# Three reorderings between VectorE and GpSimd in a one-core float32 network: the scan loop of the Mamba stage, the last mix of two mixers, the last mean square

## The reference

```
uA = head_rms_norm(oA, hg_norm_g) * silu(hz)
uB = head_rms_norm(oB, ret_norm_g) * silu(rz)
m  = sigmoid(ga) * uA + sigmoid(gb) * uB
x  = x + gate * (m @ w_out)
out = rms_norm(x, final_g)
```

```
y = y_diag + y_off + d_skip * xs
y = y * silu(z)                        # then a norm over each group of 256 channels
```

## Time and profile before

| | us |
|---|---|
| median of 3 runs | 1345.24 (1345.16 to 1345.25) |
| the profiled execution's own time | 1344.97 |
| its span | 1343.2 |
| PE busy | 1331.4 |
| DVE, ACT, POOL busy | 958.1, 753.4, 213.1 |

### The profile page before, as it was taken

The page is one execution under the profiler, slowest core; times in us unless marked ns, Lnnn a source line. Parts: engine busy times, 40 slices in busy tenths (PEclk is TensorE's granted clock), DMA queues, the critical chain, the costliest instruction groups (busy, mean ns, idle before and its releaser), DMA issues.

```text
span 1343.2 us, 21456 instructions
## 1 busy us (share of the span) xinstructions
PE 1331.4 (99%) x8527; PEld 1156.6 (86%) x8527; DVE 958.1 (71%) x1026; ACT 753.4 (56%) x882; POOL 213.1 (16%) x199
## 2 busy tenths in 40 slices
PE   9999999999999999999999999999999999999997
PEld 7888888888888888888899988888888899888886
DVE  6666668867666676666677999767888756877586
ACT  6444455656444454444566678854444465657453
POOL 3400001101000020000000026220000001655740
PEclk9999999999999999999999999999999999999999
DMA  8655546525555565555544564488887544655341
GB/s 279 209 188 189 195 159 208 188 92 191 187 187 187 188 189 189 187 187 187 188 157 162 188 207 172 145 278 294 286 285 236 187 158 157 220 160 184 113 156 49
DMA packets 158292, 254.19 MB, mean 189 GB/s; under 512 B 8784, under 2 KB 99232, under 8 KB 156560
## 3 DMA queue, kind: packets, MB, share of 16 engines
q1 hardware_dynamic: 155136, 232.94, 53.1%
q0 software_dynamic: 2576, 18.45, 3.7%
q10 hardware_dynamic: 512, 1.85, 0.4%
HBM read 252.12 MB, written 1.08 MB: 189 GB/s over the span
## 4 chain that ended last, share of the span: by engine, by line
PE 89%; issue 7%; DVE 2%; ACT 1%; DMA 1%; POOL 0%; POOLq 0%; DVEq 0%; ACTq 0%
PE psum L656 24%; PE psum L644 13%; PE psum L688 5%; PE psum L689 5%; PE psum L690 5%; PE psum L1951 4%; PE psum L1952 4%; PE psum L1953 4%; PE psum L428 3%; PE psum L429 3%; PE psum L435 3%; PE psum L463 1%; PE psum L471 1%; PE psum L465 1%; PE psum L1496 1%
## 5 line engine op out<-in xcount | busy, mean ns | idle before, releaser
L391 DVE TENSOR_TENSOR w_lo<-raw,w_hi 128x2048 fp32r<-128x2048 f32 x220 | 512.3, 2331 | 203.2 <-ACT w_hi L383 203.0
L383 ACT ACTIVATE w_hi<-raw 128x2048 fp32r<-128x2048 f32 x220 | 420.6, 1912 | 173.1 <-PE psum L690 78.5
L656 PE MATMUL psum<-hT,w_hi 128*128 128x512 f32 x1408 | 335.9, 390 | 0.6 <-DVE hT L527 0.4
L656 PEld LDWEIGHTS psum<-hT,w_hi 128*128 128x128 f32 x1408 | 260.7, 188 | 53.8 <-issue 1.2
L644 PEld LDWEIGHTS psum<-hT,w_lo 128*128 128x128 f32 x1408 | 180.2, 191 | 6.6
L644 PE MATMUL psum<-hT,w_lo 128*128 128x256 f32 x1408 | 183.0, 283 | 0.0
L688 PE MATMUL psum<-w_hi,hidT_hi 128*128 128x512 f32 x320 | 125.1, 391 | 0.0
L689 PE MATMUL psum<-w_lo,hidT_hi 128*128 128x512 f32 x320 | 125.0, 391 | 0.0
L690 PE MATMUL psum<-w_hi,hidT_lo 128*128 128x512 f32 x320 | 124.5, 389 | 0.0
L533 POOL TENSOR_SCALAR meansq<-sumsq 128x2 f32<-128x2 f32 x7 | 5.9, 836 | 659.8 <-ACT xn L501 659.8
L738 ACT ACTIVATE hid<-psum 128x512 f32<-128x512 f32 x44 | 26.3, 598 | 149.8 <-PE psum L644 149.8
(11 more groups left out here) (387 smaller groups left out, 1996.6 us busy)
## 6 DMA issues: line engine op xcount, KB each, us to landing
raw<-in_ffn_w_up SPq DMA_DIRECT2D x88, 512.0 KB, 4.8
raw<-in_ffn_w_down SPq DMA_DIRECT2D x88, 512.0 KB, 4.3
raw<-in_ffn_w_gate SPq DMA_DIRECT2D x86, 512.0 KB, 4.7
raw<-in_w_in SPq DMA_DIRECT2D x72, 512.0 KB, 4.6
raw<-in_ssm_w_in SPq DMA_DIRECT2D x48, 512.0 KB, 4.6
raw<-in_attn_w_qkv SPq DMA_DIRECT2D x24, 512.0 KB, 4.7
ada_in<-in_w_ada POOLq DMA_DIRECT2D x8, 1536.0 KB, 8.3
raw<-in_ssm_w_out SPq DMA_DIRECT2D x16, 512.0 KB, 4.3
```

The source lines that it names most:

```text
L383: act.activation(w_hi[:, slot, :], raw[:, slot, :], ACT.Copy).then_inc(sem("hi_ready"), 1)
L391: dve.tensor_tensor(w_lo[:, slot, :], raw[:, slot, :], w_hi[:, slot, :].bitcast(F32), ALU.subtract)\
L656: pe.matmul(both, hi[:, k, at_:at_ + P], hT[:, k, :, :], start=k == 0, stop=False, skip_group_check=True)
```

## The change

- Start: `first_lo` no longer raises a semaphore for its first three pieces, on which nothing waited.
- Scan loop, DVE: in pair j = 1 the `split_lo` stands behind the weighing and no longer ahead of the finishing.
- Scan loop, POOL: the second of the two early gatings of y is issued at item 11, behind that item's `xdt` and `x_skip`, and no longer at item 10.
- Last mix, DVE: out_b is multiplied by gate_b for both halves at once, behind the head squares of tick 25 (`gate_second`) and ahead of the head factors and the sigmoid. `mix` is then: out_b by the sigmoid, out_a plus out_b. The head factors for the second half are applied in tick 26, ahead of that tick's split, and no longer in tick 27.
- Last mean: DVE adds the two sums of squares and epsilon in one instruction for each token half, and POOL only takes the power.

```diff
--- before.py
+++ after.py
@@ -1015,8 +1015,7 @@
                     dve.wait_ge(sem("first_hi"), k + 1)
                 else:
                     dve.wait_ge(sem("hi_ready"), 1)
-                dve.tensor_tensor(w_lo[:, 0, cs], raw[:, 0, cs], w_hi[:, 0, cs].bitcast(F32), ALU.subtract)\
-                   .then_inc(sem("first_lo" if k < 3 else "lo_ready"), 1)
+                return dve.tensor_tensor(w_lo[:, 0, cs], raw[:, 0, cs], w_hi[:, 0, cs].bitcast(F32), ALU.subtract)
 
             hT_lo_tiles(dve, 0, ("ffn1_norm", 0), (0, 1))
             first_lo(0)
@@ -1024,7 +1023,7 @@
             hT_lo_tiles(dve, 0, ("ffn1_norm", 0), (2, 3))
             first_lo(2)
             hT_lo_tiles(dve, 0, ("ffn1_norm", 0), (4, 5))
-            first_lo(3)
+            first_lo(3).then_inc(sem("lo_ready"), 1)
             hT_lo_tiles(dve, 0, ("ffn1_norm", 0), (6, 7))
             split_lo(dve, 1)
             split_lo(dve, 2)
@@ -1734,8 +1733,8 @@
                     load_cum(1)
                 if i == 10:
                     group_rstd(0)
-                if i in (7, 10):
-                    q = (i - 7) // 3
+                if i in (7, 11):
+                    q = (i - 7) // 4
                     cs = slice(512 * q, 512 * (q + 1))
                     pool.wait_ge(sem("y"), 4 * (q + 1))
                     pool.wait_ge(sem("z_silu"), q + 1)
@@ -1864,11 +1863,14 @@
             for j in range(1, ITEMS // 2):
                 differences(2 * j)
                 differences(2 * j + 1)
-                split_lo(dve, FIRST_UNIT["ssm_z"] + j - 1 + SLOTS)
+                if j > 1:
+                    split_lo(dve, FIRST_UNIT["ssm_z"] + j - 1 + SLOTS)
                 finish(2 * j - 2)
                 finish(2 * j - 1)
                 weigh(2 * j)
                 weigh(2 * j + 1)
+                if j == 1:
+                    split_lo(dve, FIRST_UNIT["ssm_z"] + SLOTS)
                 if j == 6:
                     lo_of_y(0)
             split_lo(dve, FIRST_UNIT["ssm_z"] + ITEMS // 2 - 1 + SLOTS)
@@ -2289,13 +2291,9 @@
             head_rstd_pool(pool, 1)
             pool.wait_ge(sem("gained"), 4)
             pool.dma_start(gain_row[:, :], w["final_g_2"][0].partition_broadcast(P)).then_inc(sem("gain_in"), 16)
-            order = in_order(pool, "gpsimd_order")
-            pool.wait_ge(sem("sumsq"), 4 * 7 + 2)
-            order(pool.tensor_scalar(meansq[:, :], sumsq[:, 0, :], 1.0, EPS, ALU.mult, ALU.add))
             for t in range(TT):
                 ts = slice(t, t + 1)
-                pool.wait_ge(sem("sumsq"), 4 * 7 + 2 + t + 1)
-                order(pool.tensor_tensor(meansq[:, ts], meansq[:, ts], sumsq[:, 1, ts], ALU.add))
+                pool.wait_ge(sem("mean"), t + 1)
                 pool.tensor_tensor(rstd[:, ts], meansq[:, ts], neg_half[:, ts], ALU.pow).then_inc(sem("rstd"), 1)
 
         def across_tokens(row):
@@ -2366,13 +2364,14 @@
                 if i < TICKS - 2:
                     second_dve_tick(dve, i)
                 c = NT + i // 2
+                if i == TICKS - 2:
+                    normed(dve, 1, out_b, None, (1,))
                 if i == TICKS - 1:
                     lo_of_m(dve, 0)
-                    normed(dve, 1, out_b, None, (1,))
                     mix(dve, c, 1)
                 split_lo(dve, u + 2 * NT + i + SLOTS)
                 if i % 2 and GA <= CHUNKS2[c] < GB:
-                    gate(dve, c)
+                    gate_first(dve, c)
                 if i == TICKS - 3:
                     normed(dve, 1, out_b, None, (0,))
                     mix(dve, c, 0)
@@ -2395,6 +2394,11 @@
                         dve.tensor_tensor(scaled[:, t, cs], x[:, t, cs], gain_row[:, cs], ALU.mult)\
                            .then_inc(sem("gained_x"), 1)
             for t in range(TT):
+                ts = slice(t, t + 1)
+                dve.wait_ge(sem("sumsq"), 4 * 7 + 2 + t + 1)
+                dve.scalar_tensor_tensor(meansq[:, ts], sumsq[:, 0, ts], EPS, sumsq[:, 1, ts], ALU.add, ALU.add)\
+                   .then_inc(sem("mean"), 1)
+            for t in range(TT):
                 dve.wait_ge(sem("rstd"), 8 + t)
                 dve.scalar_tensor_tensor(xn[:, t, cs], x[:, t, cs], rstd[:, t:t + 1], gain_row[:, cs],
                                          ALU.mult, ALU.mult).then_inc(sem(f"final_{t}"), 1)
@@ -2404,14 +2408,18 @@
             dve.tensor_tensor(hT_lo[:, k, :], h_tmp[:, k, :], hT_hi[:, k, :].bitcast(F32), ALU.subtract)\
                .then_inc(sem("hT"), 1)
 
-        def gate(dve, c):
-
-            n = 2 * (CHUNKS2[c] >= GB) + CHUNKS2[c] % D // 512
-            to = (gate_b if n >= 2 else gate_a)[:, :, 512 * (n % 2):512 * (n % 2 + 1)]
+        def gate_first(dve, c):
+
+            n = CHUNKS2[c] % D // 512
+            to = gate_a[:, :, 512 * n:512 * (n + 1)]
             dve.wait_ge(sem("in2_out"), c + 1)
-            if n >= 2:
-                dve.wait_ge(sem("gained"), n + 1)
             dve.tensor_tensor(to, to, sig[:, :, :], ALU.mult).then_inc(sem("gated"), 1)
+
+        def gate_second(dve):
+
+            order = in_order(dve, "vector_order")
+            dve.wait_ge(sem("gained"), 4)
+            order(dve.tensor_tensor(out_b[:, :, :], out_b[:, :, :], gate_b[:, :, :], ALU.mult))
 
         def lo_of_m(dve, half):
             for k in range(4 * half, 4 * half + 4):
@@ -2422,11 +2430,10 @@
         def mix(dve, c, half):
 
             cs = slice(512 * half, 512 * (half + 1))
-            gate(dve, c)
-            order = in_order(dve, "vector_order")
+            b = out_b[:, :, cs]
+            dve.wait_ge(sem("in2_out"), c + 1)
+            dve.tensor_tensor(b, b, sig[:, :, :], ALU.mult).then_inc(sem("gated"), 1)
             dve.wait_ge(sem("gated"), 3 + half)
-            b = out_b[:, :, cs]
-            order(dve.tensor_tensor(b, b, gate_b[:, :, cs], ALU.mult))
             dve.tensor_tensor(out_a[:, :, cs], out_a[:, :, cs], b, ALU.add).then_inc(sem("m"), 1)
 
         def normed(dve, a, buf, other, halves=(0, 1)):
@@ -2506,6 +2513,7 @@
                 normed(dve, 0, out_a, gate_a)
             if i == OUT_B + 1:
                 head_squares(dve, 1, square_b)
+                gate_second(dve)
 
         block = ctx.enter_context(nc.Block())
         FFN1 = ("ffn1_w_gate", "ffn1_w_up", "ffn1_w_down")
```

## The result

| | before | after |
|---|---|---|
| median of the runs timed side by side | 1344.82 us (1344.03 to 1345.61, 12 runs) | 1348.93 us (1346.82 to 1350.15, 12 runs) |
| ratio | 1 | 1.0029, interval 1.0021 to 1.0037 |
| profiled execution, time and span | 1344.97, 1343.2 us | 1348.74, 1346.9 us |

The kernel became slower by 4.1 us. The forecast was 1347.0, or 1.8 more than before, with 1348.0 as its upper end. So it missed: the sign was right, the size about half. The twelve times lie in two groups: four from 1346.82 to 1347.26, eight from 1348.53 to 1350.15. The profiled execution is of the upper group.

A forecast was written before the change was run, and what follows sets the result against it. PE was taken as the bound, busy 1331.4 of 1343.2 us. Loop -0.4, mix +2.2 and mean 0 gave +1.8 on 1344.97, so 1346.8; the median stands 0.27 higher, so 1347.0, range 1343.4 to 1348.0.

The forecast's parts named there:

- Start: Kernel start: three raised semaphores fewer, with nothing waiting on them, worth 0.
- POOL held up by DVE in the last mix: Last mix: DVE's added product and a split delay POOL's scale and power; first turn 2.71 us later; chance 0.62.
- The two rivals with a lower price: Last mix: POOL not held up, 1344.3 or 1343.1 us, chance 0.16; only its scale held up, 1344.9 us, chance 0.12.
- The sum of the mix, +2.2: Last mix: first turn 2.71 us later, second turn's 0.52 us stall gone; +2.2 us, bounds -0.5 and +2.4.
- The scan loop, -0.4: Scan loop: 0.86 us of possible gain less 0.5 of slips, -0.4 us; bounds a 1.6 gain and a 0.6 loss.
- A and B: Scan loop PE stalls expected to go: scores at 795.38, 0.67 us idle; outputs at 828.89, 0.34 us late.
- The cap from DVE's weighing: Scan loop's end: DVE runs without pause to the weighing ending at 843.95, so the loop gains at most 0.86 us.
- ACT's squares as its next reader, which are a pair away: Scan loop: POOL's later gating delays nobody, since its next reader on ACT comes a pair later.
- The slips: Scan loop: earlier POOL xdt products stretch DVE's differences, delaying DVE; two slips, 0.5 us in all.
- Last mean, 0: Last mean: moving additions from POOL to DVE leaves the end unchanged, 0, between -0.1 and +0.15 us.
- The slower rival: Scan loop becomes DVE's limit through slips in pairs 2 to 6: +2.7 us or more, 1347.9 to 1348.3; chance 0.10.
- stall C: Last mix: PE idles 0.52 us before the second turn at 1318.23; expected to go, -0.52 us.

The follow-up runs named there:

- one-operand: Changed kernel with the out_b by gate_b product replaced by two tensor_reduce of gate_b, similar length, one operand read, output lacking that factor: 1345.24 us.
- gate-behind: Changed kernel with the out_b by gate_b product put behind tick 25's split, so POOL makes the head factors first: 1346.27 us.
- mix alone: Kernel before with only the last mix's edits, scan loop and mean as before: 1347.14 us; profiled again three times.
- the kernel with the ten matmuls: Changed kernel plus ten 128x512 matmuls whose result nobody reads, put on PE ahead of the wait for the first turn: 1347.51 us.
- copy-first kernel: scan-only kernel with ACT's last copy of z ahead of the second quarter's squares instead of behind them: 1345.61 us.
- scan-only kernel: Kernel before with only the scan loop's two edits (weighing ahead of split, gating behind item 11's xdt): 1345.90 us.
- loop-all kernel: copy-first kernel with pair 7's two DVE splits moved back, behind item 15's weighing and behind its finish: 1344.09 us.

## Why the prediction was wrong

- **Start**: it was not run alone; nothing of it was seen in the kernels that hold it.
- **POOL held up by DVE in the last mix** (the forecast's main case): right. Scale 2.17 (forecast some 2.2), power 4.97 (over 4), its end 1308.90 (1308.70), idle at the first turn 2.51 (some 2.7), no idle at the second. The two rivals with a lower price fell in the profile, and the one-operand and gate-behind kernels show the cause, with one operand fewer or with POOL first.
- **The sum of the mix, +2.2**: mis-sized, and this is the step that failed most. It took the 2.7 us of idle as lost time and nothing more, and kept the matmuls behind it at their durations of before. In three of five profiles with that idle TensorE's clock fell to 0.50 behind it, for another 1.6 us, in the profile of the changed kernel too. By the times, eight of twelve executions of the changed kernel and five of eleven of the mix alone would be of that kind. Without it the term is 2.2, as the lower group of the mix alone shows, and 2.1 by its trace (the first turn 2.71 later, counted from the second output unit, and 7.77 instead of 8.40 from turn to turn). The upper edge of the range was drawn from stalls alone, so it did not hold 1348.9. The four executions of the lower group (1346.82 to 1347.26) lie inside it and near the forecast of 1347.0, but with a loop term of the wrong sign that is luck.
- **The scan loop, -0.4**: wrong in sign, +1.2 by the time of the loop alone and +0.8 by the positions. A and B did go, but their 1.0 us was the figure of one execution, and others of the same loop have 0.34 to 1.13. The cap from DVE's weighing is real, as the copy-first kernel shows, but it was not reached: PE met ACT's copies of z first, the last one in all six profiles with the gating moved and ACT's order as before, and the one before it in four of these. The step "ACT's squares as its next reader, which are a pair away" looked at who reads the gated quarter and not at what else stands in ACT's order. The slips were also put on the wrong engine. Beside the early `xdt` the differences kept their 2.18 us, and it was POOL's `xdt` that took 3.35 (at 796.91, 2.60 before). What PE lost came by the same way at the end: POOL's scale, then `x_skip` of item 15, for a second stall. The prediction named a stall at items 14 and 15 as the sign that DVE limits the loop; the stall behind them came from POOL waiting for DVE, which is another thing.
- **Last mean, 0**: right, within what can be measured.
- **The slower rival** named the scan loop as the place and 1347.9 to 1348.3 as the price. Its place was right in part, the mechanism was not, and the clock was in no case.

Of the 4.1 us the parts explain 1.2 for the loop and 2.5 for the mix, 3.7 together; the rest is within the scatter of the runs. In the two profiles, 3.8 us apart, the loop has 0.7 of it, the first turn 2.66 and the clock with the vanished stall C 0.97; against that the loop begins 0.45 earlier. One thing doesn't fit: the lower group of the changed kernel is 2.25 above the kernel before, where loop and mix without the clock would make 3.4 by the times and 2.9 by the traces (the kernel with the ten matmuls, which has just these two, is at +2.8). Why is open; none of its four executions has a profile. What decides whether the clock falls in an execution is not shown by these runs; that the changed kernel seems to have it more often than the mix alone (8 of 12, 5 of 11) rests on too few executions to mean anything.

## What to carry to other kernels

Ahead of a product placed into a gap of one engine, look at what a neighbour does in that gap: here POOL's 16 values per partition, 0.21 us of work, needed 2.17 beside it, and the chain behind them stood still. Price an idle of the engine that bounds the kernel at more than its length (here 2.5 us, and 1.6 more in three of five profiles), and keep such an engine busy where an idle can't be avoided. Read a stall that is to be removed in more than one execution: this one of 0.67 us was nothing in two of seven. And when a stall is removed early in a tightly packed stage, follow each engine's own order to the stage's end: A and B were 1.0 us, and 1.96 us of other stalls took their place (0.49 + 0.85 + 0.62 in the scan-only kernel), until the copy of z and two splits were moved as well.

## What the runs showed of the hardware

- The granted clock fell behind an idle of only 2.51 to 2.54 us, in an execution with TensorE at 99% of its span, once the matmuls had begun again, and stayed at 0.50 for 3.4 us in each of the three profiles that have it. An idle of the same length, within 0.03 us, left it at 1.00 in two other executions. After 0.85 us it stayed at 1.00 in the one profile taken, and the eleven times show no second group.
- DVE's instructions back to back can leave POOL no entry between them: in the changed kernel the scale of 4 values per partition, begun at 837.26, ended at 841.09 with the split that followed the differences (838.75 + 2.28). When instead an instruction with one operand in PSUM followed the differences (loop-all kernel, `finish` at 838.76), it ended with the differences, after 0.72. The Trainium skill (SBUF — State Buffer, Who interferes with whom) says that a DVE instruction with at most one input in SBUF, outside its two-port modes, doesn't contend with GpSimd; this pair of rows agrees.
- But the same POOL scale took 0.30 or 0.31 in eight profiles, begun inside the same eight instructions of DVE, and 3.82 or 3.83 in six, at the same offset in DVE's stream. Which of the two it is follows from an edit 12 us earlier on POOL, and by what way stays open.
